# A sum of squares over the partitions, moved from TensorE to GpSimd in the second mixer of a two-layer trunk

## The chip, the cores and the metric

The kernel runs on one core of a Trainium2 chip. The metric is the device time of one execution in microseconds (us). TensorE (PE) multiplies matrices, VectorE (DVE) and ScalarE (ACT) work elementwise, GpSimd (POOL) is a further engine, and SyncE (SP) issues nearly all transfers. Each engine works through its own program in order; semaphores order the engines among each other.

## What is computed

A trunk of two layers over 256 tokens of width 1024, all in float32. Each layer is a mixer and then a hierarchical mixture of experts. The second layer's mixer is a Mamba-2 scan over eight groups of 256 channels. Its end is what the change touches:

```python
def mamba2_mixer(h, in_proj, conv_w, conv_b, dt_bias, a_log, d_skip, norm_w, out_proj):
    ...
    y = ssd_scan(xs, dt, a, b_mat, c_mat)
    y = y + d_skip.astype(jnp.float32).reshape(SSM_GROUPS, SSM_HPG)[:, :, None] * xs
    y = y.reshape(bsz, seq, D_INNER) * jax.nn.silu(z.astype(jnp.float32))
    yg = y.reshape(bsz, seq, SSM_GROUPS, D_INNER // SSM_GROUPS)
    yg = yg * lax.rsqrt(jnp.mean(yg * yg, axis=-1, keepdims=True) + RMS_EPS)
    y = yg.reshape(bsz, seq, D_INNER) * norm_w.astype(jnp.float32)
    return y.astype(h.dtype) @ out_proj
```

The mean of `yg * yg` over a group's 256 channels is the quantity in question. The last step of the whole program is a root-mean-square norm of the residual over all 1024 channels.

## The kernel before

The program runs in four stages: first mixer, first mixture of experts, second mixer, second mixture of experts. Every engine has its program written out by hand, and semaphores (by name) tie them together.

The second mixer treats the eight groups as eight units, g = 0 to 7. Channels lie on the partitions and the 256 tokens along the free dimension, so a group is two tiles of 128 partitions by 256. TensorE's order for unit g is: `odd_scores(g)` (two products and four transposes, lines 2069 to 2073), `odd_z(g)` (the gate's projection, 16 products, line 1495), `odd_y(g)` (the scan's product, lines 2082 and 2083), `odd_out(g - 2)` (output projection of an earlier unit, 16 products, line 1526, from unit 2 on), `odd_x(g + 1)` (the next unit's x projection, 16 products), `odd_ss(g)` (line 2088), and `odd_bc(g + 2)` (16 products). In unit 6 `odd_out(4)` comes behind `odd_ss(6)`. Units 0 and 1 have no output projection, so there `odd_x` follows `odd_y` directly. After unit 7 come `odd_out(6)` and `odd_out(7)`. A float32 product is two matrix instructions in the trace.

VectorE closes a unit in `odd_gate(g)`: it adds the skip term, multiplies by the gate, squares, and adds the two tiles' squares into `sq[:, 0, :]` (line 1411, semaphore `yz_done`). `odd_ss(g)` multiplies that tile by a 128x128 matrix of ones, which leaves the sum over the partitions in every partition of the PSUM bank `wb` (semaphore `yss_done`). VectorE then does `odd_bc_silu(g + 1)` (line 1352), `odd_segments(g + 1)` (eight operations, line 1376), `odd_mean(g)` (line 1415, reads `wb`, semaphore `yms_done`), `odd_x_taps(g + 1)` (six operations, line 1332, behind ScalarE's first tap), `odd_mix(g)` (a Newton step and the norm's product, lines 884 to 886, 1420 and 1425) and `odd_x_silu(g + 1)` (line 1344); in the last step, from unit 6 to 7, `odd_x_silu(7)` comes ahead of `odd_mix(6)`. The next unit's `odd_scores` waits for that `odd_x_silu`. ScalarE does `odd_decay(g + 1)`, then `odd_x_tap(g + 1)` as soon as the x projection is done, then `odd_rstd(g)` (which waits for `yms_done`), then the x exponentials. ScalarE's operations all have line 588, that of a helper.

`odd_scores(g)` also writes `wb`, by its transposes, and so waits for `yms_done` of the unit before.

GpSimd sets constants in the first microseconds (lines 550 to 573) and then does nothing until the end, where `st[:, 4, t] = st[:, 5, t] ** -0.5` for the final norm runs on it, once per half of the tokens (line 579, after `mean_sq`).

Of the kernel before, what the change touches and what calls it, by code (L numbers as in the profile page):

```python
# [8 lines left out]
ALU = mybir.AluOpType  # L9
# [3 lines left out]
P = 128  # L13
# [3 lines left out]
SEQ = TT * P  # L17
EVEN_UNITS = 4
ODD_UNITS = 8
# [28 lines left out]
EPS = 1e-6  # L48
# [52 lines left out]
def trunk_program(nc, x, e_v, e_qk, e_ch, e_gb, e_out, o_z, o_x, o_bc, o_out, norm_in, params_in,  # L101
                  expert_w_gate, expert_w_up, expert_w_down, final_norm, out):
    with ExitStack() as ctx:
        def sb(name, shape, dt=F32):
            return ctx.enter_context(nc.sbuf_tensor(name, shape, dt))

        def ps(name, shape):
            return ctx.enter_context(nc.psum_tensor(name, shape, F32))

        S = {n: ctx.enter_context(nc.semaphore(n)) for n in SEMS}  # L110
# [34 lines left out]
        ones = sb("ones", [P, P])  # L145
# [44 lines left out]
        def carve(limit):  # L190
            at = [0]

            def take(*shape, rows=P):
                n = 1
                for k in shape:
                    n *= k
                v = arena[0:rows, at[0]:at[0] + n]
                at[0] += n
                assert at[0] <= limit, at[0]
                if len(shape) == 2:  # L200
                    v = v.rearrange("p (a b) -> p a b", a=shape[0])
                if len(shape) == 3:
                    v = v.rearrange("p (a b c) -> p a b c", a=shape[0], b=shape[1])
                return v
            return take

        take = carve(XDN)
# [9 lines left out]
        take = carve(ARENA)  # L218
# [9 lines left out]
        yz, sq = take(2, SEQ), take(2, SEQ)  # L228
        raw = arena[:, 0:KC * SEQ].rearrange("p (k s) -> p k s", k=KC)
        dsR = sq[0:HEADS + 1, 0, :]  # L230
        ms, rg, rt = take(SEQ), take(SEQ), take(SEQ)
        csT = rt[0:HEADS, :]
        dtv, dta, csn = (take(TT, HEADS) for _ in range(3))
        w0 = take(HEADS)

        take = carve(DN3)
        cols = take(6, NE)
# [54 lines left out]
        pa, pb, wa, wb = (ps(n, [P, 512]) for n in ("pa", "pb", "wa", "wb"))  # L292
# [254 lines left out]
        @block.gpsimd  # L547
        def _(pool):
            chain = Chain(pool, S["pool_chain"])
            nc.gpsimd.memset(zero_bf[:, :], 0.0).then_inc(S["consts_pool"], 1)  # L550
            nc.gpsimd.memset(ones[:, :], 1.0)
            nc.gpsimd.memset(one_c[:, :], 1.0)
            nc.gpsimd.memset(minus_half[:, :], -0.5)
            nc.gpsimd.memset(eps_c[:, :], EPS)
            nc.gpsimd.memset(ident[:, :], 0.0)
            nc.gpsimd.memset(later[:, :, :], 0.0)
            nc.gpsimd.iota(iota[:, :], pattern=[[1, NE]], base=0, channel_multiplier=0,
                           allow_small_or_imprecise_dtypes=True)
            nc.gpsimd.iota(iota1[:, :], pattern=[[1, NE]], base=FAR + 1, channel_multiplier=0,
                           allow_small_or_imprecise_dtypes=True)  # L560
            nc.gpsimd.memset(esum[:, 0:NG + NE], 0.0)
            nc.gpsimd.memset(esum[:, NG + NE:], 1.0 / D)
            nc.gpsimd.iota(descend[:, :], pattern=[[-1, NE]], base=NE, channel_multiplier=0,
                           allow_small_or_imprecise_dtypes=True)
            for q in range(4):
                chain.link(nc.gpsimd.iota(slot_id[32 * q:32 * q + 32, :], pattern=[[0, 1]], base=FAR + 1,
                                          channel_multiplier=1, allow_small_or_imprecise_dtypes=True))
            nc.gpsimd.affine_select(out=ident[:, :], in_=ident[:, :], compare_op=ALU.not_equal, fill=1.0,
                                    base=0, pattern=[[-1, P]], channel_multiplier=1)
            nc.gpsimd.affine_select(out=upper[:, :], in_=ones[:, :], compare_op=ALU.is_ge, fill=0.0,  # L570
                                    base=0, pattern=[[1, P]], channel_multiplier=-1)
            for b in (0, 2):
                ins = nc.gpsimd.affine_select(out=later[:, b, :], in_=later[:, b, :], compare_op=ALU.is_gt, fill=-BIG,
                                              base=0, pattern=[[-1, P]], channel_multiplier=1)
            ins.then_inc(S["consts_pool"], 1)

            for t in range(TT):
                pool.wait_ge(S["mean_sq"], t + 1)
                nc.gpsimd.tensor_tensor(st[:, 4, t:t + 1], st[:, 5, t:t + 1], minus_half[:, t:t + 1], ALU.pow
                                        ).then_inc(S["rstd"], 1)  # L580
# [296 lines left out]
        def _(dve):  # L877
            chain = Chain(dve, S["dve_chain"])
            v = nc.vector
# [532 lines left out]

            def odd_mean(g):
                dve.wait_ge(S["yss_done"], g + 1)
                v.tensor_scalar(ms, wb[:, 0:SEQ], 1.0 / 256, EPS, ALU.mult, ALU.add).then_inc(S["yms_done"], 1)

            def odd_mix(g):
                dve.wait_ge(S["yguess"], g + 1)
# [66 lines left out]
        def _(pe):  # L1485
            mm = nc.tensor.matmul
# [505 lines left out]
            def odd_bc(g):  # L1992
                pe.wait_ge(S["c2_in"], g * 16 + 16)
                if g == 1:
                    pe.wait_ge(S["bc_conv"], 1)
                else:
                    pe.wait_ge(S["z1_silu"], g - 1)
                project(bcs[g][:, 0:SEQ], w_c[2], 0)
                project(bcs[g][:, SEQ:], w_c[2], 1).then_inc(S["bc_done"], 1)

            def odd_x(g):
                pe.wait_ge(S["c1_in"], g * 16 + 16)
                pe.wait_ge(S["bc_conv"], g + 1)
                project(xz[g][:, 0:SEQ], w_c[1], 0)
                project(xz[g][:, SEQ:], w_c[1], 1).then_inc(S["x1_done"], 1)

            def odd_z(g):
                pe.wait_ge(S["c0_in"], g * 16 + 16)
                pe.wait_ge(S["x1_conv"], g + 1)
                project(xz[g][:, 0:SEQ], w_c[0], 0)  # L2010
                project(xz[g][:, SEQ:], w_c[0], 1).then_inc(S["z1_done"], 1)
# [8 lines left out]
            for n, b in enumerate((2, 3, 0, 1)):  # L2020
# [4 lines left out]
                for k in (2 * b, 2 * b + 1):  # L2025
                    ins = mm(wb[HEADS:HEADS + 1, 0:SEQ], esum[:, NG + NE:], hsq[:, k, :],
                             start=(k == 4), stop=(k == 3))
# [10 lines left out]
            for t in range(TT):  # L2038
                ins = mm(wb[:, SEQ + P * t:SEQ + P * t + P], st[:, 4, t:t + 1].to_broadcast([P, P]), ident[:, :],
                         start=True, stop=True)  # L2040
# [19 lines left out]
            def odd_scores(g):  # L2060
                pe.wait_ge(S["bc_silu"], g + 1)
                pe.wait_ge(S["x1_silu"], g + 1)
                if g:
                    pe.wait_ge(S["yms_done"], g)
                else:
                    pe.wait_ge(S["cs_copied"], 1)
                    pe.wait_ge(S["cum_used"], 1)
                bt, ct = bcT[:, 0, :], bcT[:, 1, :]
                mm(wa[:, 0:SEQ], bt[:, 0:P], ct, start=True, stop=True)
                mm(wa[:, SEQ:384], bt[:, P:], ct[:, P:], start=True, stop=True).then_inc(S["cb_done"], 1)  # L2070
                for t in range(TT):
                    for j in range(2):
                        ins = nc.tensor.transpose(wb[:, 256 * t + P * j:256 * t + P * j + P],
                                                  xT[:, j, P * t:P * t + P], ident[:, :])
                ins.then_inc(S["xst_done"], 1)

            def odd_y(g):
                pe.wait_ge(S["xdt_done"], g + 1)
                for r in range(HPG):
                    o = wa[HD * (r % 2):HD * (r % 2) + HD, 256 * (r // 2):256 * (r // 2) + 256]  # L2080
                    c = slice(HD * r, HD * r + HD)
                    mm(o, xdt[:, 0, c], decay0[:, r, :], start=True, stop=False, skip_group_check=True)  # L2082
                    ins = mm(o[:, P:], xdt[:, 1, c], decay1[:, r, :], start=False, stop=True, skip_group_check=True)
                ins.then_inc(S["y_done"], 1)

            def odd_ss(g):
                pe.wait_ge(S["yz_done"], g + 1)
                mm(wb[:, 0:SEQ], ones[:, :], sq[:, 0, :], start=True, stop=True).then_inc(S["yss_done"], 1)

            def odd_out(g):  # L2090
                pe.wait_ge(S["mix1_done"], g + 1)
                out_project(mix1[g % 2], g)

            for g in range(ODD_UNITS):
                odd_scores(g)
                odd_z(g)
                odd_y(g)
                if 2 <= g != ODD_UNITS - 2:
                    odd_out(g - 2)
                if g + 1 < ODD_UNITS:  # L2100
                    odd_x(g + 1)
                odd_ss(g)
                if g == ODD_UNITS - 2:
                    odd_out(g - 2)
                if g + 2 < ODD_UNITS:
                    odd_bc(g + 2)
# [80 lines left out]
```

## Time and profile before

| | us |
|---|---|
| median of three executions | 1261.11 (1260.34 to 1261.70) |
| the profiled execution's own time | 1262.24 |
| its span, first to last instruction | 1260.4 |
| TensorE busy in the span | 1036.2 (82%) |
| VectorE busy | 478.1 (38%) |
| ScalarE busy | 239.4 (19%) |
| GpSimd busy | 4.2, 26 instructions |

The span is what the trace shows; the execution's own time is 1.8 us longer. TensorE's busy time has modelled ends. The transfers read 459.38 MB, 365 GB/s over the span.

### The profile page before, as it was taken

Reading aid. Unit: us, or ns where it says so; the run is one execution under the profiler, and the core shown is the slowest. Engines: PE = TensorE matmul, PEld = TensorE weight load, DVE = VectorE, ACT = ScalarE, POOL = GpSimd, SP = SyncE. Lnnn points to the kernel's source line nnn. Section 1 sums busy time; section 2 is a strip of 40 time slices with the busy share of each in tenths; the row PEclk is TensorE's granted clock in tenths of the full one; section 3 lists DMA queues with packets and bytes.
Section 4 is the critical chain, followed back from the end, with each engine's and each line's share of the span. In section 5 each row is a group of like instructions: output and inputs, shape, how many; then the busy total and the mean of one; then the engine's idle time right before and its main releaser. Section 6 shows DMA issues by size and latency. Waiting matters only on the chain.

```text
span 1260.4 us, 22334 instructions
## 1 busy us (share of the span) xinstructions
PE 1036.2 (82%) x9518; PEld 703.7 (56%) x9518; DVE 478.1 (38%) x1217; ACT 239.4 (19%) x538; POOL 4.2 (0%) x26
## 2 busy tenths in 40 slices
PE   9999999776757585889999999999967675858577
PEld 7888665443334252548888888866533342424243
DVE  2351643432222222336755556473433222222213
ACT  2330211111111111113333333121111111111101
POOL 0000000000000000000000000000000000000000
PEclk9999998878788787999999999998987877879779
DMA  9929799999999999994465553999999999999996
GB/s 391 421 109 383 277 430 424 430 425 430 426 430 426 430 427 430 425 407 142 180 250 218 217 220 152 386 357 427 425 427 427 427 430 426 430 427 429 428 426 275
DMA packets 44521, 461.49 MB, mean 366 GB/s; under 512 B 4736, under 2 KB 4768, under 8 KB 14496
## 3 DMA queue, kind: packets, MB, share of 16 engines
q1 hardware_dynamic: 44256, 460.44, 88.3%
q8 instruction: 50, 0.82, 0.3%
q14 instruction: 23, 0.19, 0.0%
q10 hardware_dynamic: 192, 0.05, 0.0%
HBM read 459.38 MB, written 1.08 MB: 365 GB/s over the span
## 4 chain that ended last, share of the span: by engine, by line
PE 55%; DMA 41%; issue 1%; ACT 1%; SPq 1%; DVE 1%; POOL 0%; POOLq 0%; DVEq 0%; ACTq 0%
DMA front<-in_expert_w_up 36%; PE pa L1495 10%; PE pa L1785 10%; PE pb L1495 8%; PE wa L1785 5%; PE acc L1526 4%; PE wb L1817 3%; DMA w_x<-in_expert_w_up 3%; DMA w_dn<-in_expert_w_down 3%; PE acc L1648 2%; PE pb L1569 1%; PE pb L1741 1%; PE acc L1827 1%; ACT arena L588 1%; PE wa L2082 1%
## 5 line engine op out<-in xcount | busy, mean ns | idle before, releaser
L1785 PE MATMUL pa<-front,arena 128*32 128x256 f32 x1792 | 127.3, 447 | 82.4 <-DMA front<-in_expert_w_up 82.4
L1252 DVE TENSOR_SCALAR later<-later 128x128 f32<-128x128 f32 x64 | 14.4, 225 | 422.3 <-ACT later L588 422.3
L1785 PE MATMUL wa<-front,arena 128*32 128x256 f32 x1232 | 99.3, 490 | 88.8 <-DMA front<-in_expert_w_up 85.3
L1785 PEld LDWEIGHTS pa<-front,arena 128*32 128x32 f32 x1792 | 63.5, 128 | 148.7 <-DMA front<-in_expert_w_up 94.8
L1785 PEld LDWEIGHTS wa<-front,arena 128*32 128x32 f32 x1232 | 47.3, 139 | 143.8 <-DMA front<-in_expert_w_up 95.7
L588 ACT ACTIVATE arena<-wb 32x256 f32<-32x256 f32 (+1 forms) x232 | 86.9, 375 | 103.7 <-PE wb L1817 95.4
L1817 PE MATMUL wb<-w_dn,later 128*32 128x256 f32 x1472 | 87.9, 380 | 1.3 <-DMA w_dn<-in_expert_w_down 1.2
L1495 PE MATMUL pa<-hnT,w_x 128*128 128x256 f32 x384 | 85.1, 380 | 0.0
L1785 PE MATMUL wa<-w_x,arena 128*32 128x256 f32 x896 | 64.4, 451 | 18.8 <-DMA w_x<-in_expert_w_up 18.8
L1495 PEld LDWEIGHTS pa<-hnT,w_x 128*128 128x128 f32 x384 | 72.6, 190 | 9.8 <-issue 0.3
L1495 PE MATMUL pb<-hnT,w_x 128*128 128x256 f32 x336 | 74.5, 380 | 0.0
L1741 PE MATMUL pb<-arena 32*128 32x512 f32 x128 | 71.7, 640 | 0.0
L588 ACT ACTIVATE later<-wa 128x128 f32<-128x128 f32 x32 | 8.9, 277 | 320.7 <-PE wa L1785 320.7
L1495 PEld LDWEIGHTS pb<-hnT,w_x 128*128 128x128 f32 x336 | 63.5, 190 | 8.6 <-issue 0.4
L1817 PEld LDWEIGHTS wb<-w_dn,later 128*32 128x32 f32 x1472 | 46.7, 110 | 36.2 <-issue 3.6
L588 ACT ACTIVATE arena<-arena 128x512 f32<-128x512 f32 (+5 forms) x84 | 54.4, 660 | 63.5 <-DVE arena L1376 29.0
L588 ACT ACTIVATE later<-pa 128x128 f32<-128x128 f32 x32 | 8.8, 275 | 300.2 <-PE pa L1785 300.2
L1785 PEld LDWEIGHTS wa<-w_x,arena 128*32 128x32 f32 x896 | 33.3, 129 | 53.5 <-issue 40.2
L1183 DVE TENSOR_SCALAR arena<-pb,slot_id 128x256 f32<-128x256 f32 x64 | 30.7, 480 | 84.1 <-PE acc L1827 63.6
L1253 DVE RECIPROCAL later<-later 128x128 f32<-128x128 f32 x64 | 61.0, 953 | 2.2
L1827 PE MATMUL acc<-arena 128*128 128x256 f32 x224 | 52.1, 386 | 8.4 <-ACT arena L588 8.4
L1526 PE MATMUL acc<-arena,w_x 128*128 128x256 f32 x256 | 57.7, 382 | 0.0
(330 smaller groups left out, 1240.7 us busy)
## 6 DMA issues: line engine op xcount, KB each, us to landing
w_dn<-in_expert_w_down SPq DMA_DIRECT2D x46, 2048.0 KB, 26.3
front<-in_expert_w_gate SPq DMA_DIRECT2D x42, 2048.0 KB, 20.7
front<-in_expert_w_up SPq DMA_DIRECT2D x42, 2048.0 KB, 25.2
w_x<-in_expert_w_gate SPq DMA_DIRECT2D x15, 2048.0 KB, 31.4
w_x<-in_expert_w_up SPq DMA_DIRECT2D x15, 2048.0 KB, 35.8
arena<-in_expert_w_down SPq DMA_DIRECT2D x14, 2048.0 KB, 26.9
front<-in_expert_w_up SPq DMA_DIRECT2D x10, 1024.0 KB, 8.5
w_x<-in_o_bc SPq DMA_DIRECT2D x8, 1024.0 KB, 6.8
```

What stands on the lines that cost most here:

```text
L588: return nc.scalar.activation(*a, **k)
L1183: link(v.tensor_scalar(G4[b], B_ps[:, 0:SEQ], slot_id[:, :], None, ALU.is_equal))
L1252: link(v.tensor_scalar(eg, eg, 1.0, None, ALU.add))
L1253: link(v.reciprocal(eg, eg))
L1495: ins = mm(dst, w[:, k, j, :], hnT[:, k, :], start=(k == 0), stop=(k == KC - 1))
L1526: ins = mm(acc[:, b, 256 * i:256 * i + 256], w[:, j, 256 * b + P * i:256 * b + P * i + P], m[:, j, :], start=(u == 0 and i == 0 and j == 0 ...
L1569: ins = mm(bank[:, t, :], hnT[:, k, P * t:P * t + P], we_v[:, i, k, :], start=(k == 0), stop=(k == KC - 1))
L1648: ins = mm(acc[:, b, 256 * i:256 * i + 256], we_o[:, b, j, P * i:P * i + P], mixA[:, j, :], start=(i == 0 and j == order[0]), stop=(j == o ...
L1741: mm(B_ps[:, :], sel, PG, start=True, stop=True).then_inc(S["b_done"], 1)
L1785: ins = mm(gu[32 * j:32 * j + 32, :, :], xb[:, k, c0:c0 + CAP], w[k][:, :, P * j:P * j + P], start=(k == 0), stop=(k == KC - 1))
L1817: ins = mm(y[32 * c:32 * c + 32, :], ht[:, 32 * j:32 * j + 32], rows[j][:, 256 * b:256 * b + 256], start=(j == 0), stop=(j == 3))
L1827: ins = mm(acc[:, b, 256 * i:256 * i + 256], a, m, start=False, stop=False, skip_group_check=True)
```

## The change

The sum over the partitions of `sq[:, 0, :]` is made by GpSimd's `partition_all_reduce`, which writes it into every partition of a new SBUF tile `yss` (128x256). GpSimd's program gets one such operation per unit, each behind `yz_done` of its unit and `yms_done` of the unit before. TensorE's `odd_ss` is gone with its wait for `yz_done`, and `odd_scores(g)` no longer waits for `yms_done`. `odd_mean` reads `yss` in place of the PSUM bank.

```diff
@@ tiles
         w0 = take(HEADS)
+        yss = take(SEQ)
@@ GpSimd's program, behind the constants
+            for g in range(ODD_UNITS):
+                pool.wait_ge(S["yz_done"], g + 1)
+                if g:
+                    pool.wait_ge(S["yms_done"], g)
+                nc.gpsimd.partition_all_reduce(yss, sq[:, 0, :], P, bass.bass_isa.ReduceOp.add).then_inc(S["yss_done"], 1)
+
             for t in range(TT):
                 pool.wait_ge(S["mean_sq"], t + 1)
@@ VectorE's program
             def odd_mean(g):
                 dve.wait_ge(S["yss_done"], g + 1)
-                v.tensor_scalar(ms, wb[:, 0:SEQ], 1.0 / 256, EPS, ALU.mult, ALU.add).then_inc(S["yms_done"], 1)
+                v.tensor_scalar(ms, yss, 1.0 / 256, EPS, ALU.mult, ALU.add).then_inc(S["yms_done"], 1)
@@ TensorE's program
             def odd_scores(g):
                 pe.wait_ge(S["bc_silu"], g + 1)
                 pe.wait_ge(S["x1_silu"], g + 1)
-                if g:
-                    pe.wait_ge(S["yms_done"], g)
-                else:
+                if not g:
                     pe.wait_ge(S["cs_copied"], 1)
                     pe.wait_ge(S["cum_used"], 1)
...
-            def odd_ss(g):
-                pe.wait_ge(S["yz_done"], g + 1)
-                mm(wb[:, 0:SEQ], ones[:, :], sq[:, 0, :], start=True, stop=True).then_inc(S["yss_done"], 1)
-
...
                 if g + 1 < ODD_UNITS:
                     odd_x(g + 1)
-                odd_ss(g)
                 if g == ODD_UNITS - 2:
                     odd_out(g - 2)
```

TensorE's order from the output projection of unit 2 to the scores of unit 3, before (line 1526 is the output projection, 1495 the x and then the B and C projection):

```order
L1526 MATMUL acc<-arena,w_x 128x256 x15
L1495 MATMUL pa<-hnT,w_x 128x256 [waits bc_conv,c1_in]
L1495 MATMUL pa<-hnT,w_x 128x256 x15
L2088 MATMUL wb<-arena,ones 128x256 [waits yz_done]
L1495 MATMUL pb<-hnT,w_x 128x256 [waits z1_silu,c2_in]
L1495 MATMUL pb<-hnT,w_x 128x256 x15
L2069 MATMUL wa<-arena 128x256 [waits yms_done,x1_silu,bc_silu]
```

The same place now (the line numbers are seven, further down five higher):

```order
L1533 MATMUL acc<-arena,w_x 128x256 x15
L1502 MATMUL pa<-hnT,w_x 128x256 [waits bc_conv,c1_in]
L1502 MATMUL pa<-hnT,w_x 128x256 x15
L1502 MATMUL pb<-hnT,w_x 128x256 [waits z1_silu,c2_in]
L1502 MATMUL pb<-hnT,w_x 128x256 x15
L2074 MATMUL wa<-arena 128x256 [waits x1_silu,bc_silu]
```

One product and its wait are gone between the two projections, and the scores wait for two semaphores in place of three.

GpSimd's order now, from the last constants to the end:

```order
L574 AFFINE_SELECT later<-later 128x128 x2
L582 ISA
L582 ISA arena<-arena 128x256 [waits yz_done]
L582 ISA arena<-arena 128x256 [waits yms_done,yz_done] x7
L586 ISA
L586 TENSOR_TENSOR st<-st,minus_half 128x1 [waits mean_sq] x2
```

## Rows read from the trace of the kernel before

**Rows 1.** Busy time by stretch: from:to, us, PE, PEld, DVE, ACT, POOL, clock, DMA share, GB/s.

```profile
582.00:814.00 232.00, 230.80 (x1158) 199.81 (x1156) 138.45 (x333) 77.67 (x124) 0.00 (x0) 1.00 0.60 224
814.00:900.00 86.00, 81.30 (x961) 53.62 (x964) 43.83 (x135) 16.86 (x44) 0.00 (x0) 0.96 0.98 401
```

**Rows 2.** Chain of waits, pieces in order of time: start us, us, what.

```profile
662.19 0.43 PE wb L2088 x2
662.62 6.91 PE pb L1495 x32
669.53 0.43 PE wa L2069 x2
...
803.50 10.36 PE acc L1526 x48
```

**Rows 3.** Timeline, unit 0 to 1, last row 6 to 7: start, us, operation, idle before.

```profile
602.55 0.42 DVE L1411 TENSOR_TENSOR arena<-arena 128x256 f32<-128x256 f32 x1
602.90 0.68 DVE L1352 TENSOR_TENSOR arena<-arena 128x512 f32<-128x512 f32 x1
...
606.40 0.42 DVE L1415 TENSOR_SCALAR arena<-wb 128x256 f32<-128x256 f32 x1 [0.98 <-PE wb L2088]
606.84 1.00 ACT L588 ACTIVATE arena<-pa,params 128x256 f32<-128x256 f32 x2
...
607.88 2.68 DVE L1332 SCALAR_TENSOR_TENSOR arena<-pa,params,arena 128x255 f32<-128x255 f32 x6 [1.05 <-ACT arena L588]
...
612.98 0.69 DVE L1344 TENSOR_TENSOR arena<-arena 128x512 f32<-128x512 f32 x1
...
613.76 0.67 PE L2069 MATMUL wa<-arena 128*128 128x256 f32 x2 [0.50 <-issue]
...
786.22 0.67 PE L2069 MATMUL wa<-arena 128*128 128x256 f32 x2 [0.20 <-issue]
```

**Rows 4.** Timeline, unit 2 to unit 3.

```profile
651.91 0.43 DVE L1411 TENSOR_TENSOR arena<-arena 128x256 f32<-128x256 f32 x1
...
662.66 0.42 DVE L1415 TENSOR_SCALAR arena<-wb 128x256 f32<-128x256 f32 x1 [7.89 <-PE wb L2088]
...
663.28 2.68 DVE L1332 SCALAR_TENSOR_TENSOR arena<-pa,params,arena 128x255 f32<-128x255 f32 x6 [0.20 <-ACT arena L588]
...
668.38 0.69 DVE L1344 TENSOR_TENSOR arena<-arena 128x512 f32<-128x512 f32 x1
...
669.37 0.59 PE L2069 MATMUL wa<-arena 128*128 128x256 f32 x2
```

**Rows 5.** Timeline, unit 7 to the end of the mixer.

```profile
799.69 0.42 DVE L1411 TENSOR_TENSOR arena<-arena 128x256 f32<-128x256 f32 x1
...
803.53 0.42 DVE L1415 TENSOR_SCALAR arena<-wb 128x256 f32<-128x256 f32 x1 [3.42 <-PE wb L2088]
...
806.59 0.88 DVE L1425 SCALAR_TENSOR_TENSOR arena<-arena,params 128x256 f32<-128x256 f32 x2
```

**Rows 6.** One size of the mean's operation; GpSimd's groups; the final norm's timeline.

```profile
L886 DVE TENSOR_SCALAR arena<-arena 128x256 f32<-128x256 f32 x8 | 2.3, 294 | 0.3
```

```profile
L570 POOL TENSOR_SCALAR_AFFINE_SELECT upper<-ones 128x128 f32<-128x128 f32 x1 | 0.3, 293 | 0.0
...
L554 POOL MEMSET eps_c<- 128x1 f32 x1 | 0.1, 98 | 0.0
```

```profile
1254.05 0.16 DVE L1460 SCALAR_TENSOR_TENSOR st<-st 128x1 f32<-128x1 f32 x1
1254.29 0.55 POOL L579 TENSOR_TENSOR st<-st,minus_half 128x1 f32<-128x1 f32 x1 [1250.22 <-DVE st L1460]
...
1255.14 0.72 ACT L588 ACTIVATE w_x<-w_x,st 128x512 f32<-128x512 f32 x1
```

**Rows 7.** A table load (ScalarE's groups), and transfer issues of the page: KB, us to landing.

```profile
L590 ACT ACT_TABLE_LOAD x1 | 1.3, 1283 | 0.8 <-PEq L2173 0.8
```

```profile
w_x<-in_o_bc SPq DMA_DIRECT2D x8, 1024.0 KB, 6.8
```

## The prediction

> **What bounds the kernel where the change acts.** I read the busy time by stretch first. In the second mixer (582 to 814 us) TensorE is busy 230.80 of 232 us at the full granted clock, the transfers take 0.60 of their engines, and GpSimd does nothing [rows 1]. Look there for the engine with no room left. The chain of waits says the same by name: its pieces from one unit to the next are all TensorE's, and the product with ones is one of them, 0.43 us between the x projection and the 6.91 us of the B and C projection [rows 2]. From 814 to 900 us TensorE is still busy 81.30 of 86 us [rows 1], so I take each microsecond that the mixer ends earlier or later as one microsecond of the program.
>
> Then I read the timeline at three places, because "TensorE is full" hides how near the other engines are. The reader should follow one loop: x projection done, ScalarE's first tap, VectorE's six taps, exponentials and mix, x silu, scores.
>
> - From unit 0 to 1 the scores start at 613.76, with 0.50 us of idle time before them, 0.09 us after the x silu ended (612.98 + 0.69 = 613.67) [rows 3]. Here TensorE already waits for that loop. The step from unit 1 to 2 looks the same, that from 6 to 7 shows 0.20 us [rows 3].
> - From unit 2 to 3 the scores start at 669.37 without idle time, but the x silu ended at 668.38 + 0.69 = 669.07 [rows 4]: the loop is only 0.21 us (669.37 - 669.07 - 0.09) from being the bound. Units 3 to 5 repeat this.
> - After unit 7 the two output projections follow, and the second needs the mix of unit 7, which ends at 806.59 + 0.88 = 807.47 [rows 5].
>
> **The change, part by part.**
>
> *TensorE's product goes.* Eight times 0.43 us [rows 2] is 3.4 us, the most the change can bring. I don't count all of it. At the steps from units 0, 1 and 6 the loop through the x silu sets the scores, and it starts at the end of the x projection, ahead of the removed product, so it does not move: gain 0. At the steps from units 2 to 5 the scores can come 0.21 us earlier before they meet the loop: 4 x 0.21 = 0.84. Behind unit 7 the full 0.43 is there if the mix is in time. Together 1.27 us. The dropped wait for `yms_done` brings nothing: VectorE's mean stands ahead of the x silu in its own order, so the scores still can't pass it.
>
> *GpSimd's reduction comes in.* Let T be the time from the end of line 1411 to the start of VectorE's mean. The mean now reads SBUF, and I give it 0.29 us, as line 886 takes for the same size [rows 6], against 0.42. The mean stands ahead of the x taps on VectorE; a late mean holds the taps, the mix, the x silu, and so the scores. Deadlines:
>
> - Steps from units 0, 1, 6: line 1411 ends at 602.97 and the taps start at 607.88 [rows 3]; T up to 607.88 - 0.29 - 602.97 = 4.6 us is free. Each microsecond beyond is paid, three times.
> - Steps from units 2 to 5: line 1411 ends at 652.34, the taps start at 663.28 [rows 4]. T up to 10.6 us is free, because an output projection lies between. VectorE now idles 7.89 us there.
> - Unit 7: line 1411 ends at 800.11; from the mean's start to the end of the mix it was 807.47 - 803.53 = 3.94 us [rows 5], now 3.81; with 0.09 to TensorE the last projection can start at 804.01 + T. Before it started at 803.50 + 6.91 = 810.41, the projection being 32 of the 48 instructions of its piece [rows 2, 5]. So T up to 6.0 keeps the 0.43, and beyond 6.4 it costs T - 6.4.
>
> *How long is T?* No such operation is in the trace; it must be bounded. The handover is there: the small power on GpSimd costs 1255.14 - (1254.05 + 0.16) = 0.93 us from VectorE's end to its user's start [rows 6]. GpSimd's elementwise pass over 128 columns takes 293 ns against 98 for one column, 1.52 ns a column, so 0.39 us for 256 columns [rows 6]. Low end: one pass in and one out, 0.93 + 0.78 = 1.7 us. High end: 127 additions of one partition after another, each a pass, 0.93 + 127 x 0.39 = 50 us. Between ends so far apart I take the count that a tree needs, nearest to the one pass that the trace shows: seven halvings of 128 partitions, seven steps to bring the sum back to all, one pass in and one out, 16 x 0.39 + 0.93 = 7.2 us, where the middle in ratio of the ends would be 9.2.
>
> A rule is weighed against this. Right behind line 1411 VectorE runs line 1352 for 0.68 us with two SBUF inputs, then the eight operations of line 1376 with one [rows 3]. The Trainium skill ("SBUF — State Buffer", on the shared port pair) says that a VectorE instruction with two SBUF inputs and a GpSimd instruction that reads SBUF exclude each other for the whole of whichever is first. By that rule each reduction would start about 0.6 us later and the sum would be 2.4 us more. The trace of before has no two such instructions at once, so I leave it out of the sum.
>
> *The sum at T = 7.2.* 3 x (7.2 - 4.6) = 7.8; unit 7: 0.8; gain at units 2 to 5: -0.84. Together +7.8 us. The step from 5 to 6 is of the second kind and is in the four. On the profiled execution's 1262.24 this gives 1270.0; its own time stands 1.1 above the median of 1261.11, which I take as the base: 1268.9.
>
> *The two unnamed rows on GpSimd* (the sets of operations made ready) are taken at nothing. They have no wait, so the first should run at 4 us, 600 us before its use, and the second at some 820 us, 440 us before the final norm. This cover is idle time of GpSimd itself. *Transfers:* the mix of unit 7 also releases weight transfers of the second mixture, now some 4 us later. The chain of waits before passes by TensorE there, not by transfers, so I add nothing; the transfers' share of 0.98 over 814 to 900 us [rows 1] says that this cover is thin, and the range has to hold what it may cost.
>
> **The rivals.**
>
> 1. *The reduction is short and hides* (not slower). T below 4.6 us: every deadline holds, and -1.27 us gives 1259.8. It needs no more than nine passes. For it: the two-pass bound of 1.7 us. Against: the sum crosses partitions, which no GpSimd operation of this trace does. The other side of the forecast's sign begins at T = 5.0, where three late steps eat the 1.27 us.
> 2. *The reduction is long*, beyond 10.6 us, and all eight units pay. At the middle in ratio of 10.6 and 50, T = 23: 3 x 18.4 + 16.6 + 4 x 12.4 = 121 us, so 1382. TensorE would then idle in each unit while the x taps wait. For it: the 50 us bound. The Trainium skill ("GPSIMD Engine Reference", cross-partition) gives 247.7 us for a reduction over the partitions at 128x2048; an eighth of that, my estimate from the page, is 31 us, and the sum by it would be some +175 us. That is another instruction, and no row here tells whether this one shares its pace.
> 3. *Making the sets ready is not hidden.* If the load is done only when the first operation behind it is called, unit 0 and the final norm each pay it, on the chain. Bounds from rows: a table load on ScalarE, 1.28 us, and the landing of 1024 KB, 6.8 us [rows 7]: 2.6 to 13.6 us on top of 7.8, so 1271.5 to 1282.5. For it: the two rows stand exactly there. Against: they carry no wait. The Trainium skill ("GPSIMD Engine Reference", instruction dispatch) says that the first call to a freshly loaded kernel pays about 6 us that no profiled instruction shows; by that figure, an estimate, the sum is 12 us more.
> 4. *The loop is looser than I read* and the 3.4 us come back in full with a short T: 1257.7.
>
> **How the numbers follow.** Forecast (T from 4.6 to 10.6) 0.42, with its own range from 1259.8 (T = 4.6) to 3 x 6.0 + 4.2 - 0.84 = +21.4, so 1282.5; rival 1: 0.20; rival 2: 0.25; rival 3: 0.10; rival 4: 0.03. A measurement of this kernel can tell 0.2%, some 2.5 us, from no change. Slower by more needs 3 x (T - 4.6) - 1.27 above 2.5, T above 5.9. So "same" is rival 1 and the sixth of the forecast below 5.9: 0.27. "Faster" is rival 4: 0.03. "Slower" is the rest: 0.70. The range starts just below rival 1, at 1259.3, and reaches into rival 2 up to T = 18 (3 x 13.4 + 11.6 + 4 x 7.4 = 81 us, 1342); about half of rival 2 lies beyond it, and rival 4 below.
>
> **What the profile after would show.** The gap between the end of line 1411 and the start of the mean is T itself. At the steps from units 0, 1 and 6 VectorE's mean should end T - 4.6 behind its old place and TensorE idle before the scores by that much more than now; at units 2 to 5 the mean should be done before the first tap ends, with some 0.2 us of idle time before the scores. Rival 3 would show as a gap of several us between `mean_sq` and the power on GpSimd near the end, and a longer T in unit 0 than in unit 1. I am wrong in the mechanism if the mixer's length does not follow T by these deadlines, and wrong in size only if it does with another T.

## The result, and the profile after

The changed kernel takes 1266.36 us (median of 6 executions, 1264.24 to 1268.51) against 1260.83 before in the same comparison: ratio 1.0044, 95% interval 1.0033 to 1.0055, so 5.5 us slower. The profiled execution took 1268.22 with a span of 1266.5, 6.1 us more than the span before.

GpSimd now shows the eight reductions. This is the timeline from unit 0 to unit 1 in the changed kernel, the place of [rows 3] (line 1418 closes the squares, 1359 is the B and C silu, 1383 the segments, 1422 the mean, 1339 the x taps, 1351 the x silu, 2074 the scores; ScalarE's first row is the decay exponential, its second the first tap):

```profile
603.00 0.42 DVE L1418 TENSOR_TENSOR arena<-arena 128x256 f32<-128x256 f32 x1
603.35 0.68 DVE L1359 TENSOR_TENSOR arena<-arena 128x512 f32<-128x512 f32 x1
603.57 2.21 POOL L582 PARTITION_ALL_REDUCE arena<-arena  x1 [599.22 <-DVE arena L1418]
603.95 3.01 DVE L1383 TENSOR_SCALAR arena<-arena 128x256 f32<-128x256 f32 x8
...
606.88 0.28 DVE L1422 TENSOR_SCALAR arena<-arena 128x256 f32<-128x256 f32 x1
606.99 1.48 ACT L595 ACTIVATE arena<-arena 128x1536 f32<-128x1536 f32 x1 [5.23 <-DVE arena L1383]
608.38 1.00 ACT L595 ACTIVATE arena<-pa,params 128x256 f32<-128x256 f32 x2
...
609.42 2.69 DVE L1339 SCALAR_TENSOR_TENSOR arena<-pa,params,arena 128x255 f32<-128x255 f32 x6 [2.26 <-ACT arena L595]
...
614.51 0.68 DVE L1351 TENSOR_TENSOR arena<-arena 128x512 f32<-128x512 f32 x1
...
615.35 0.88 PE L2074 MATMUL wa<-arena 128*128 128x256 f32 x2 [2.06 <-DVE arena L1351]
```

Read it downward. The reduction is over about 605.8, long before anything needs it. But the eight segment operations beside it take 3.01 us. Before they took 1.92 (1.91 once) in all eight units. The place in the kernel before, with the rows that [rows 3] leaves out (ScalarE's is the decay exponential):

```profile
603.50 1.92 DVE L1376 TENSOR_SCALAR arena<-arena 128x256 f32<-128x256 f32 x8
605.45 1.48 ACT L588 ACTIVATE arena<-arena 128x1536 f32<-128x1536 f32 x1 [4.14 <-DVE arena L1376]
605.76 0.59 PE L2088 MATMUL wb<-arena,ones 128*128 128x256 f32 x2
```

Some of the eight are stretched, as line 1383 (1376 before) shows by its shortest, median and longest duration in ns, here of the changed kernel and then of the one before:

```profile
L1383 DVE TENSOR_SCALAR arena<-arena x64: 273/308/1187, 586.5 to 784.7; 128x256 f32<-128x256 f32 x32, 128x128 f32<-128x128 f32 x32
```

```profile
L1376 DVE TENSOR_SCALAR arena<-arena x64: 279/314/350, 586.1 to 777.9; 128x256 f32<-128x256 f32 x32, 128x128 f32<-128x128 f32 x32
```

In unit 0's step it is two of the eight: the first, at 603.95, takes 1184 ns, the second 342 again, and the third 600. The extra time, 0.84 + 0.26 us, is the 1.09 us that all eight lose. The second and third, in a view of the stretch that holds these two:

```profile
L1383 DVE TENSOR_SCALAR arena<-arena x2: 342/471/600, 605.1 to 605.3; 128x256 f32<-128x256 f32 x2
```

ScalarE's decay exponential waits for the segments, and the first tap stands behind it in ScalarE's queue: it starts at 608.38, though the x projection was done at 606.2. Taps, silu and scores follow, and TensorE idles 2.06 us. In unit 7, where no segments follow, the reduction is bare:

```profile
807.09 1.79 POOL L582 PARTITION_ALL_REDUCE arena<-arena  x1 [23.27 <-DVE arena L1418]
808.91 0.29 DVE L1422 TENSOR_SCALAR arena<-arena 128x256 f32<-128x256 f32 x1 [1.92 <-POOL arena L582]
```

T, from the end of line 1418 to the start of the mean, is 1.92 us there.

The gap has a second price. Busy time by stretch in the changed kernel (columns as in [rows 1]; the clock is the third from the right):

```profile
613.30:615.30 2.00, 0.00 (x0) 0.00 (x0) 1.86 (x4) 0.86 (x3) 0.00 (x0) 1.00 0.60 113
615.30:617.50 2.20, 2.15 (x9) 2.07 (x10) 0.69 (x3) 1.01 (x2) 0.00 (x0) 0.59 0.93 389
617.50:620.00 2.50, 2.50 (x10) 2.04 (x9) 2.39 (x4) 0.00 (x0) 0.00 (x0) 0.68 0.52 208
620.00:623.00 3.00, 3.00 (x16) 2.64 (x15) 2.63 (x7) 0.00 (x0) 0.00 (x0) 1.00 0.00 0
```

In the 2.2 us after a gap of 2.06 us TensorE's granted clock averages 0.59 of 2.4 GHz. Taken in stretches of 1 us it is 0.50, the lower level of 1.2 GHz, from 616.3 to 618.3, and it is back at the upper one by 620. From the scores to the end of the gate's projection it takes 625.29 - 615.35 = 9.94 us, before 622.04 - 613.76 = 8.28. The same happens one unit later (0.54 from 642.80 to 645.20). After the gap of 1.77 us ahead of unit 7's scores it does not.

The steps between the starts of the scores hold nearly the whole account, in us (from the timelines' rows of lines 2069 and 2074):

| step | 0 to 1 | 1 to 2 | 2 to 3 | 3 to 4 | 4 to 5 | 5 to 6 | 6 to 7 | sum |
|---|---|---|---|---|---|---|---|---|
| before | 24.67 | 24.68 | 30.93 | 30.85 | 30.84 | 30.85 | 24.31 | 197.13 |
| changed | 25.81 | 27.49 | 32.44 | 30.77 | 30.76 | 30.77 | 25.52 | 203.56 |

The sum grows by 6.4. Behind unit 7 the stretch to the first product of the router (the second mixture of experts) shrinks from 27.47 to 27.04 us, the product's 0.43. Together that is +6.0 of the span's 6.1. Outside these stretches unit 0's scores start 0.45 us later (589.54 against 589.09) and the part behind the first router product is 0.35 us shorter. Nothing of the change acts there.

### The profile page after: what moved, and what is told of

Its sections match the earlier page's. It is cut to its first block, busy times and chain, and to the rows that moved or that the text cites. A ratio compares the mean times of both kernels' runs of the same rounds, so it can differ in the third digit from the quotient of the medians.

```text
span 1266.5 us, 22321 instructions
## 1 busy us (share of the span) xinstructions
PE 1040.6 (82%) x9502; PEld 703.4 (56%) x9502; DVE 484.0 (38%) x1217; ACT 239.4 (19%) x538; POOL 21.8 (2%) x34
## 4 chain that ended last, share of the span: by engine, by line
PE 51%; DMA 41%; DVE 4%; ACT 2%; issue 1%; SPq 1%; POOLq 0%; POOL 0%; DVEq 0%; ACTq 0%
DMA front<-in_expert_w_up 38%; PE pa L1792 10%; PE pa L1502 8%; PE pb L1502 7%; PE wa L1792 5%; PE acc L1533 4%; PE wb L1824 3%; DMA w_x<-in_expert_w_up 3%; PE acc L1655 2%; ACT arena L595 2%; PE pb L1576 1%; PE pb L1748 1%; PE acc L1834 1%; DVE arena L1383 1%; PE pb L1868 1%
## 6 DMA issues: line engine op xcount, KB each, us to landing
w_dn<-in_expert_w_down SPq DMA_DIRECT2D x46, 2048.0 KB, 26.4
```

## The experiments

**Theory.** The reduction and the segments' first operations exclude each other at SBUF; the late segments go through ScalarE's queue to the tap; the gap then costs clock. **Rivals:** the reduction's length T, as predicted; or the removed product itself. All times are medians. The ratio is to the kernel before, run beside each experiment, with a median of 1261.58 to 1261.66.

**1. The reduction waits for the segments** (e1).

```diff
                 if g:
                     pool.wait_ge(S["yms_done"], g)
+                if g + 1 < ODD_UNITS:
+                    pool.wait_ge(S["seg_done"], g + 2)
```

> The changed kernel, but GpSimd's reduction of units 0 to 6 also waits until VectorE's eight segment operations are done. Theory (the reduction, which takes 1.9 us, shuts VectorE out of its first segment operation for 0.9 us; the late segments hold ScalarE's decay exponential, and that holds the first tap queued behind it): segments back to 1.92 us, first tap of units 1, 2, 7 back at its place, no idle time of TensorE above 1 us and no fall of its clock; the mean starts about 1.9 us behind the segments, inside its deadline; time about 1260 to 1261, some 5.5 us under the changed kernel. Rival (the reduction's own length T is what is paid, as predicted): T grows by 2.4 us, so three steps get later by up to 2.4 us each and the time rises to 1270 or more. Rival (the missing product or wait on TensorE): no change, 1266.

1261.1 us, ratio 0.9998 (0.9989 to 1.0007). The whole loss is gone though T has grown. Its timeline from unit 0 to 1:

```profile
604.40 1.92 DVE L1385 TENSOR_SCALAR arena<-arena 128x256 f32<-128x256 f32 x8
606.35 1.48 ACT L597 ACTIVATE arena<-arena 128x1536 f32<-128x1536 f32 x1 [4.15 <-DVE arena L1385]
606.54 1.81 POOL L584 PARTITION_ALL_REDUCE arena<-arena  x1 [602.20 <-DVE arena L1385]
...
608.39 0.29 DVE L1424 TENSOR_SCALAR arena<-arena 128x256 f32<-128x256 f32 x1 [2.07 <-POOL arena L584]
...
614.71 0.67 PE L2076 MATMUL wa<-arena 128*128 128x256 f32 x2 [0.98 <-DVE arena L1353]
```

T is now 608.39 - 603.88 = 4.5 us, just inside the deadline of 4.6 that the prediction worked out. The steps sum to 196.96 us, as in the kernel without any sum (experiment 3), so the reduction costs nothing here. In the changed kernel T is shorter, 606.88 - 603.42 = 3.5 us in unit 0 (the mean stands behind the late segments), and the time is longer. T was not what the change paid.

**2. The reduction as a passenger** (e2). The kernel before with TensorE's product, and the reduction added unused:

```diff
+            for g in range(ODD_UNITS):
+                pool.wait_ge(S["yz_done"], g + 1)
+                if g:
+                    pool.wait_ge(S["par_done"], g)
+                nc.gpsimd.partition_all_reduce(yss, sq[:, 0, :], P, bass.bass_isa.ReduceOp.add).then_inc(S["par_done"], 1)
@@ odd_mean
+                dve.wait_ge(S["par_done"], g + 1)
                 dve.wait_ge(S["yss_done"], g + 1)
```

> The kernel before, with TensorE's product with ones kept, and GpSimd's reduction added beside it, its result used by nobody (VectorE's mean waits for both). Theory (GpSimd's reading disturbs VectorE): the full loss of the change shows without the change's other parts, about +6 to +7.5 us on 1260.8, first segment operation 1.18 us in units 0 to 6. Rival (the reduction's length or the missing product): 1261 within noise, because the mean has its sum from TensorE and waits for GpSimd no longer than T = 1.9 us.

1265.26 us, ratio 1.0029 (1.0017 to 1.0040): slower, as the theory says, but by 3.6 us and not by 6 to 7.5. The segments take 3.01 us again:

```profile
603.82 3.01 DVE L1383 TENSOR_SCALAR arena<-arena 128x256 f32<-128x256 f32 x8
...
606.86 1.49 ACT L595 ACTIVATE arena<-arena 128x1536 f32<-128x1536 f32 x1 [5.24 <-DVE arena L1383]
608.25 1.00 ACT L595 ACTIVATE arena<-pa,params 128x256 f32<-128x256 f32 x2
...
615.18 0.67 PE L2077 MATMUL wa<-arena 128*128 128x256 f32 x2 [1.59 <-issue]
```

The product with ones fills 0.43 us of the gap, which is now 1.59, and the scores keep their 0.67 us: the clock does not fall (1.00 from 615.1 to 620). The seven steps sum to 200.43 us, 3.3 more than before, and behind unit 7 it is 28.00 against 27.47. I had missed that the removed product was also what kept the gap short.

**3. No sum at all** (e3). The mean reads the squares of one partition each; the sum over the partitions is left out.

```diff
-                dve.wait_ge(S["yss_done"], g + 1)
-                v.tensor_scalar(ms, yss, 1.0 / 256, EPS, ALU.mult, ALU.add).then_inc(S["yms_done"], 1)
+                dve.wait_ge(S["yz_done"], g + 1)
+                v.tensor_scalar(ms, sq[:, 0, :], 1.0 / 256, EPS, ALU.mult, ALU.add).then_inc(S["yms_done"], 1)
```

> The changed kernel without any sum over the partitions: no reduction on GpSimd, none on TensorE, the mean reads the tile of squares itself (the norm's divisor is left out as a true sum). It prices the removed product alone. By the prediction's count: 0.84 for the four middle steps and 0.43 behind unit 7, so 1.27 us under the kernel before, 1259.6. Rival (the loop is looser than read): 3.4 us under, 1257.4. Rival (the product's removal itself is what hurts, through the idle time on TensorE): slower than 1260.8.

1261.3 us, ratio 0.9995 (0.9986 to 1.0004). The product's removal alone is worth 0.4 us by the medians (by the ratio's interval between 1.8 us gained and 0.5 lost), and not 3.4. The seven steps sum to 196.96 against 197.13. Behind unit 7 the 0.43 is lost again: 80 instructions of the output projections take 17.92 us in the timeline against 17.53 in the changed kernel, and the chain of waits from 800 to 825 us, here by line, passes through the transfer of the last projection's weights. In the changed kernel and in e1 that chain has no transfer. Why the transfer ends last in this run is not shown.

```profile
796.58 17.92 PE L1527 MATMUL acc<-arena,w_x 128*128 128x256 f32 x80
```

```profile
by line: PE acc L1527 45.1%; DMA w_x<-in_o_out 27.5%; PE wb L1504 13.0%; PE acc L1701 10.6%; PE wb L1509 3.8%; issue 0.6%
```

**4. The decay exponential out of the tap's way** (e4, and e9 on another occasion). ScalarE's order alone:

```diff
                     odd_rstd(g - 1)
+                    odd_decay(g)
                     odd_x(g)
...
                     odd_bc(g + 1)
-                    odd_decay(g + 1)
```

> The changed kernel with ScalarE's decay exponential moved behind the first tap and the rstd of the unit, so that late segments no longer hold the tap. Theory: VectorE still loses 0.9 us in each unit, but the tap starts when the x projection is done; the scores of units 1, 2 and 7 come 1.6 us or more earlier than in the changed kernel and the clock does not fall; time about 1258 to 1260. Rival (VectorE's own lateness is the path, not ScalarE's queue): the taps start 0.3 to 0.9 us earlier at most and the time stays at 1264 to 1266.

1257.79 us, ratio 0.9969 (0.9957 to 0.9982); the repetition gave 1258.07, 0.9973 (0.9963 to 0.9984). The segments still take 3.01 us, and it no longer matters:

```profile
606.05 1.02 ACT L595 ACTIVATE arena<-pa,params 128x256 f32<-128x256 f32 x2 [4.66 <-PE pa L1502]
...
613.03 0.67 PE L2074 MATMUL wa<-arena 128*128 128x256 f32 x2
```

So it is ScalarE's queue that carries the delay, not VectorE's own lateness: the tap starts 0.2 us behind the projection, and the scores follow it by 6.98 us. The time is also 3.9 us under the kernel before, where the tap waited for the decay exponential too. Experiment 8 takes the move and the sum apart.

**5. TensorE kept busy in the gap** (e5).

```diff
             def odd_scores(g):
+                if g in (1, 2, 7):
+                    for i in range(14):
+                        mm(wb[:, 0:SEQ], zero_bf[:, :], zero_bf[:, :].unsqueeze(1).to_broadcast([P, 2, P]), start=True, stop=True, skip_group_check=True)
```

> The changed kernel with 14 small products of zeros (bf16, 256 columns, about 1.5 us together) on TensorE ahead of the scores of units 1, 2 and 7, into a bank that the scores overwrite. Theory (the gaps of 2.06 us let the granted clock fall to the lower level, which costs 9.94 - 8.28 = 1.7 us from the scores to the end of the gate's projection in units 1 and 2): the clock stays at the upper level, the segments stay late, the scores stay late; time 3.3 us under the changed kernel, about 1263. Rival (the slow stretch has another cause, such as the transfers of that moment): products still slow, 1266.

1264.52 us, ratio 1.0024 (1.0015 to 1.0033), against 1.0044 for the changed kernel. The scores stay late, and the clock stays up; the same stretch as above, here:

```profile
613.00:615.30 2.30, 2.30 (x18) 1.73 (x16) 2.20 (x6) 1.62 (x3) 0.00 (x0) 1.00 0.69 175
615.30:617.50 2.20, 1.67 (x12) 1.58 (x12) 1.09 (x5) 1.02 (x2) 0.00 (x0) 1.00 0.86 346
617.50:620.00 2.50, 2.50 (x13) 2.22 (x12) 2.50 (x5) 0.00 (x0) 0.00 (x0) 1.00 0.69 279
```

From the first scores to the last it takes 200.21 us, 3.35 less than the changed kernel, which is the two slow stretches of 1.66. The rest, 200.21 - 197.13 = 3.1, is the lateness itself, 3.5 in three steps, less 0.4 gained in the middle ones. By the medians of two comparisons the products win back 5.5 - 2.9 = 2.6 us, not 3.3.

**6. Which VectorE form is shut out** (e7, one execution). The segments take their bound from a PSUM tile in place of the constant 0, so the clamp at 0 is left out. The operation has one SBUF input as before, but runs at the single rate. Here 128 and 256 columns take 340 and 477 ns, 1.07 ns a column; before, 279 and 350, 0.55.

```diff
-                        ins = v.tensor_scalar(d[:, r, :], csr[:, r, first:], csn[:, b, n:n + 1], 0.0,
-                                              ALU.subtract, ALU.min)
+                        ins = v.scalar_tensor_tensor(d[:, r, :], csr[:, r, first:], csn[:, b, n:n + 1],
+                                                     wb[:, 0:SEQ - first], ALU.subtract, ALU.min)
```

> The changed kernel with VectorE's segment operations in another form: a lower bound read from a PSUM tile takes the place of the constant 0 (so the clamp of the decay exponents is wrong), which leaves one SBUF input and no doubled rate. Theory (the first segment operation is shut out because it runs at the doubled rate, which takes both SBUF ports): the operations take longer without company (0.43 to 0.48 us for 256 columns) but the first one is not stretched, none above 0.6 us. Rival (any VectorE read of SBUF waits for the reduction): the first is still near 1.2 us or more.

```profile
L1383 DVE SCALAR_TENSOR_TENSOR arena<-arena,wb x64: 340/408/477, 587.0 to 781.2; 128x256 f32<-128x256 f32 x32, 128x128 f32<-128x128 f32 x32
```

No operation is stretched: the longest takes 477 ns beside the same reduction. All eight take 2.68 us and not 3.01. That is still 0.76 more than before, so the form is no remedy: the gap is 1.75 us, the clock stays up behind it, and the one execution took 1264.25 us. The Trainium skill ("VectorE: DVE Perf Modes", mode 2x_2P) says that an fp32 `tensor_scalar` from SBUF to SBUF runs at two elements a cycle by taking both SBUF ports, and ("SBUF — State Buffer", who interferes with whom) that this form contends with GpSimd while a form with one SBUF input at the single rate does not. Both traces agree, 1187 ns against 477. By that page the port is held for the whole instruction of whoever came first; here the reduction lasts 1.79 us bare, and the operation that it stretches loses 1.18 - 0.34 = 0.84, so it gets through before the reduction ends: by the records it is over at 605.13 and the reduction at 605.78, and the third segment operation is stretched by 0.26 more. The measurement does not bear out one hold over the whole reduction. What holds there are instead is not shown.

**7. The price of a column** (e8, one execution). The kernel before with an unused reduction behind the segments, 64 columns wide in unit 0, and 64 more in each unit.

```diff
+                n = 64 * g + 64
+                nc.gpsimd.partition_all_reduce(yss[:, 0:n], sq[:, :, :].rearrange("p a b -> p (a b)")[:, 0:n], P, bass.bass_isa.ReduceOp.add).then_inc(S["par_done"], 1)
```

> The kernel before with an unused reduction per unit behind the segments (no company on VectorE), 64, 128, ... 512 columns wide for units 0 to 7. It measures the price of a column. From 1.79 us at 256 columns and the 0.55 us of the small power: a slope of about 5 ns a column and a fixed 0.5 us, so about 0.9 us at 64 and 3.0 us at 512. Rival (mostly fixed cost): 1.5 us at 64 and 2.1 at 512.

```profile
607.10 0.73 POOL L585 PARTITION_ALL_REDUCE arena<-arena  x1 [602.73 <-DVE arena L1386]
631.76 1.07 POOL L585 PARTITION_ALL_REDUCE arena<-arena  x1 [23.93 <-DVE arena L1386]
...
687.27 1.79 POOL L585 PARTITION_ALL_REDUCE arena<-arena  x1 [29.41 <-DVE arena L1386]
...
802.65 3.24 POOL L585 PARTITION_ALL_REDUCE arena<-arena  x1 [19.95 <-DVE arena L1421]
```

64, 128, 256 and 512 columns: 5.6 ns a column ((3.24 - 0.73) / 448) and 0.37 us fixed. The reductions of 192, 320, 384 and 448 columns lie on the same line (1.44, 2.15, 2.51 and 2.87 us). The expected slope was 5.

**8. What each sum is worth in the better order.** e6 and e10 are the kernel before with the move of experiment 4. e11 and e12 add to e9 and e10 that VectorE's x silu comes ahead of the mix in all units:

```diff
-                    if more:
-                        odd_mix(g - 1)
                     odd_x_silu(g)
-                    if not more:
-                        odd_mix(g - 1)
+                    odd_mix(g - 1)
```

> The kernel before (TensorE's product with ones) with only ScalarE's decay exponential moved behind the first tap and the rstd. It tells how much of the 3.9 us that the changed kernel with the same move gained over the kernel before is due to the move. Theory: the move frees the steps from units 0, 1 and 6 (0.3 to 0.5 us each, what TensorE idled), so 1260.4, and the version with GpSimd's reduction is faster by the product, up to 8 x 0.43 = 3.4 us. Rival (the move is all): 1257.8, no difference between the two sums.

> The same kernel as e4, run beside the three others of this call so that they are compared on one chip. Expected 0.3% under the kernel before, as in e4.

> The same kernel as e6. With e9 it gives what GpSimd's sum is worth once the decay exponential is out of the way. Theory (the loop through the x silu takes 7.2 us from the end of the x projection, against 7.34 us of TensorE's product and B and C projection): only 0.1 to 0.2 us a step, together 1 to 2 us, not 3.4.

> e9 with VectorE's x silu ahead of the mix in all units, as unit 7 has it already. Theory: the silu no longer waits for the mix's 2.5 us, only for ScalarE's exponentials, which end some 0.3 us earlier; the scores follow the projection with less idle time, 0.1 to 0.25 us in six steps; about 1 us under e9. Rival (the loop was not the bound any more in e9): the same as e9.

> e10 with the same order on VectorE. TensorE has no idle time before its scores there (7.34 us of work against a loop of 7.2), so nothing should change against e10; the difference between e11 and e12 is then what the removed product is worth without a loop in its way, up to 3 us.

| | sum on TensorE | sum on GpSimd |
|---|---|---|
| order of before | 1 | 1.0044 (1.0033 to 1.0055) |
| decay later, on two chips | 0.9984 (0.9975 to 0.9993), e6 | 0.9969 (0.9957 to 0.9982), e4 |
| decay later, on one chip | 0.9987 (0.9978 to 0.9996), e10 | 0.9973 (0.9963 to 0.9984), e9 |
| and x silu first | 0.9982 (0.9973 to 0.9991), e12 | 0.9961 (0.9947 to 0.9975), e11 |

The move alone is worth 2.1 us (e6, 1259.48) and 1.9 us (e10, 1259.71) to the kernel before, where 1260.4 was expected for e6. Its steps from units 0, 1 and 6 shrink by 0.65, 0.74 and 0.36 us, because the first tap no longer waits for the decay exponential. So about half of what e4 gains over the kernel before is the move's. The rest is what GpSimd's sum is worth in this order: 1259.71 - 1258.07 = 1.6 us (e10 and e9). With the x silu first as well it is worth more: e11 at 1256.78 us is 2.6 us under e12 at 1259.40, on one chip, and under both kernels of the study. Against e9 and e10 the second move brings 1.3 and 0.3 us, where about 1 and nothing were expected. In e11 the silu ends at 612.77 and the scores start 0.17 us later:

```profile
612.08 0.69 DVE L1351 TENSOR_TENSOR arena<-arena 128x512 f32<-128x512 f32 x1 [2.11 <-ACT arena L595]
...
612.94 0.66 PE L2071 MATMUL wa<-arena 128*128 128x256 f32 x2
```

Its seven steps sum to 192.62 us against 195.30 in e12: 2.7 of the 7 x 0.43 = 3.0 us that the removed product holds there.

## Why the prediction was right or wrong

The number was near (+7.8 forecast, +5.5 measured) and the direction right. The mechanism was wrong: T, which was to pay all of it, paid nothing. T was put far too long, and the true costs were left out, and that the two errors nearly cancelled is luck. The prediction had named its own test, that the mixer's length follows T by the deadlines. From the changed kernel to e1 T in unit 0 goes from 3.5 to 4.5 us and the time from 5.5 us over the kernel before to 0.6 under it.

- *What bounds the mixer:* right. The lateness sits in the steps from units 0, 1 and 6, as forecast, and the middle steps have room.
- *Where the loop starts:* wrong at these three steps, though its gain of 0 for the product came. The x projection was done by 605.76, when the product with ones started, but the tap started at 606.84, behind the decay exponential. The loop ran through the segments and the decay. Where the tap does start with the projection's end (e6), the steps are 0.36 to 0.74 us shorter.
- *The price of T:* the step that failed first. Sixteen passes of 0.39 us and a handover of 0.93 gave 7.2; measured is 1.92 in unit 7, where nothing else runs. Counting one elementwise pass for each level of a tree was the main error: the whole reduction costs 5.6 ns a column, under four passes of 1.52 ns. The 0.93 also held the small power's own 0.55 us; here 1.92 - 1.79 = 0.13 is left beside the reduction. By the prediction's own deadlines T = 1.92 is free, and the sum would have been -1.27. The condition of rival 1 held, and its result did not.
- *The port:* the step that failed second. The rule was weighed, but only its half on two SBUF inputs, and the segments were passed over as "one SBUF input". The row that hints otherwise was among the rows read: line 886, the same kind of operation on 128x256, takes 294 ns [rows 6], where line 1415, which reads PSUM, takes 0.42 us [rows 3]. And I looked for the harm in the reduction's start, not in the operations beside it.
- *The path of the harm:* missed. The deadline was drawn for VectorE's mean alone. The decay exponential stands ahead of the first tap on ScalarE; before it ended at 605.45 + 1.48 = 606.93, and the tap started at 606.84 [rows 3], so that path had no slack at all. VectorE's delay of 1.1 us went straight into the loop: +1.14, +1.13 and +1.21 us in the three steps (e5, where the clock stays up).
- *The clock:* missed, 3.3 us of the 6.0 in the profiled executions. The prediction said that TensorE would idle longer before the scores and gave idle time no further price.
- *The product's gain:* 0.84 us for the middle steps was too much, 0.4 measured (30.93 + 30.85 + 30.84 + 30.85 against 32.44 less its slow 1.66, 30.77, 30.76, 30.77). The 0.43 behind unit 7 came, where the forecast at T = 7.2 had a cost of 0.8.
- *The reductions' set made ready at no cost:* right. Unit 0's reduction takes 2.21 us, those of units 1 to 6 take 2.24 to 2.25, and the final power starts 0.09 us behind its input, as before 0.08; rival 3 falls.

```profile
1260.11 0.16 DVE L1467 SCALAR_TENSOR_TENSOR st<-st 128x1 f32<-128x1 f32 x1
1260.36 0.60 POOL L586 TENSOR_TENSOR st<-st,minus_half 128x1 f32<-128x1 f32 x1 [451.48 <-DVE st L1467]
```

- *Rival 2's estimate* has a slip in its sum: at T = 31 the deadlines give 3 x 26.4 + 24.6 + 4 x 20.4 = 185 us, not 175. No reduction here comes near it: 512 columns take 3.24 us (e8).
- *Rival 4* (the 3.4 us come back in full) was wrong for this order: e3 has 0.4 us of it. With two more moves 2.6 us come back (e11 against e12).

## What to carry to other kernels

When work moves to GpSimd, look at what VectorE does at that moment, and at the rate at which it does it. Here a float32 operation on one SBUF tensor took 0.29 us for 256 columns where one with a PSUM input took 0.42, and it was the fast form that GpSimd shut out. The cost then appears in whatever waits for VectorE. Draw the deadline for every engine that the disturbed operations feed, in its queue's order, not for the new result alone. A short operation on the bounding engine can be worth less than its length where the next wait is close. It can also fill part of a gap: with it the gap was 1.59 us and the clock stayed up, without it 2.06 us and the clock fell.

## What the runs showed of the hardware that was not expected

- A sum over all 128 partitions on GpSimd, result in every partition, takes 0.37 us and 5.6 ns a column in float32 (e8; 1.79 us for 256 columns). It takes 2.2 us when it starts 0.46 us before the end of a VectorE operation with two SBUF inputs. That it waits for this operation is inferred: it also took 2.14 to 2.16 us in e7, where the segments were not stretched, and no run took line 1359 away.
- It stretches two VectorE operations at the doubled rate, the first from 0.34 to 1.18 us and the third to 0.60, but none at the single rate (e7). Behind the segments it stretches none (e1).
- TensorE's clock fell to the lower level after gaps of 2.06 and 2.07 us in these places (changed kernel) and not after gaps of 1.59 (e2), 1.75 (e7) and 1.77 us (changed kernel, unit 7); the fall cost 1.66 us each time.
